# Weights of a hybrid decoder block loaded by 1 MB for two units into two neighbouring slots, instead of 512 KB per unit

## What is computed

```
hn = rms_norm(h, mix_norm_w)
q, k, v, z, xbc, dt, gates = split(hn @ w_in)      # 2048, 2048, 2048, 4096, 6144, 64, 4096 columns
attn = causal attention of 16 heads of 128, q and k normalised per head, ALiBi bias
ssm  = causal conv of width 4 on xbc, SiLU, chunked SSD scan (2 chunks of 128), D skip, gated group RMSNorm with SiLU(z)
h = h + (sigmoid(g_a) * (attn @ w_attn_out) + sigmoid(g_s) * (ssm @ w_ssm_out)) @ w_out
h = h + relu(rms_norm(h, mlp_norm_w) @ w_up)^2 @ w_down      # 8192 wide
```

## Time and profile before

| | us |
|---|---|
| median of three runs | 2007.39 (2006.86 to 2008.67) |
| the profiled execution, its own time | 2008.35 |
| its span, first to last instruction | 2006.6 |
| TensorE busy (matmul) in it | 2000.7 |
| VectorE busy | 1271.5 |
| ScalarE busy | 1103.1 |
| GpSimd busy | 189.7 |

### The profile page before, as it was taken

One profiled execution on the slowest core, in us unless ns is written; L12 is line 12 of the kernel. 1 busy time (PEld: TensorE's weight loads), 2 busy tenths in 40 slices (PEclk: granted clock), 3 DMA queues, 4 the chain that ended last, 5 costly groups with the idle time before them and its releaser, 6 DMA issues.

```text
span 2006.6 us, 25425 instructions
## 1 busy us (share of the span) xinstructions
PE 2000.7 (100%) x9022; PEld 1659.7 (83%) x9022; DVE 1271.5 (63%) x1455; ACT 1103.1 (55%) x1250; POOL 189.7 (9%) x190
## 2 busy tenths in 40 slices
PE   9999999999999999999999999999999999999999
PEld 7888888888888888888888888888888888888887
DVE  5676676777787666666675565656546555655554
ACT  6665666667766454545774444555445435544542
POOL 2110120112221111110000000010001000000000
PEclk9999999999999999999999999999999999999999
DMA  7787887789976666665986766767666766766775
GB/s 246 204 203 197 215 205 201 215 229 240 246 218 191 193 193 197 190 197 178 231 233 197 212 203 233 211 199 211 209 194 202 225 196 191 227 202 188 212 222 164
DMA packets 324282, 417.34 MB, mean 208 GB/s; under 512 B 138832, under 2 KB 139792, under 8 KB 323936
## 3 DMA queue, kind: packets, MB, share of 16 engines
q1 hardware_dynamic: 322768, 412.62, 71.0%
q10 hardware_dynamic: 960, 2.75, 0.4%
q0 software_dynamic: 464, 0.77, 0.2%
HBM read 382.46 MB, written 2.16 MB: 192 GB/s over the span
## 4 chain that ended last, share of the span: by engine, by line
PE 99%; DMA 0%; ACTq 0%; DVE 0%; DVEq 0%; issue 0%
PE ps L610 32%; PE ps L612 32%; PE ps L611 32%; PE ps L793 1%; PE ps L579 0%; PE ps L655 0%; PE ps L678 0%; PE ps L782 0%; DMA x_in<-in_x 0%; PE ps L803 0%; PE ps L679 0%; PE ps L656 0%; PE ps L699 0%; PE ps L701 0%; PE ps L586 0%; PE ps L587 0%
## 5 line engine op out<-in xcount | busy, mean ns | idle before, releaser
L1437 DVE TENSOR_TENSOR wlo<-raw,whi 128x1024 fp32r<-128x1024 f32 x703 | 886.7, 1268 | 631.6 <-ACT whi L911 630.1
L911 ACT ACTIVATE whi<-raw 128x1024 fp32r<-128x1024 f32 x703 | 738.8, 1058 | 682.1 <-PE ps L612 663.2
L610 PE MATMUL ps<-whi,xT_hi 128*128 128x512 f32 x1276 | 505.6, 396 | 0.0
L612 PE MATMUL ps<-whi,xT_lo 128*128 128x512 f32 x1276 | 497.4, 390 | 0.0
L611 PE MATMUL ps<-wlo,xT_hi 128*128 128x512 f32 x1276 | 496.6, 389 | 0.0
L612 PEld LDWEIGHTS ps<-whi,xT_lo 128*128 128x128 f32 x1276 | 239.4, 188 | 50.8
L611 PEld LDWEIGHTS ps<-wlo,xT_hi 128*128 128x128 f32 x1276 | 239.8, 188 | 49.1 <-issue 1.0
L610 PEld LDWEIGHTS ps<-whi,xT_hi 128*128 128x128 f32 x1276 | 239.7, 188 | 48.7 <-issue 1.1
L610 PE MATMUL ps<-whi,hT_hi 128*128 128x512 f32 x512 | 199.3, 389 | 0.0
L612 PE MATMUL ps<-whi,hT_lo 128*128 128x512 f32 x512 | 199.2, 389 | 0.0
L610 PE MATMUL ps<-whi,fT_hi 128*128 128x512 f32 x512 | 199.2, 389 | 0.0
(11 more groups left out here) (263 smaller groups left out, 1907.7 us busy)
## 6 DMA issues: line engine op xcount, KB each, us to landing
raw<-in_w_in SPq DMA_DIRECT2D x319, 512.0 KB, 4.1
raw<-in_w_up SPq DMA_DIRECT2D x128, 512.0 KB, 4.3
raw<-in_w_down SPq DMA_DIRECT2D x128, 512.0 KB, 4.2
raw<-in_w_ssm_out SPq DMA_DIRECT2D x64, 512.0 KB, 4.3
raw<-in_w_attn_out SPq DMA_DIRECT2D x32, 512.0 KB, 4.3
raw<-in_w_out SPq DMA_DIRECT2D x32, 512.0 KB, 4.4
arow<-arows SPq DMA_DIRECT2D x16, 512.0 KB, 4.8
h<-in_x ACTq DMA_DIRECT2D x1, 2048.0 KB, 10.9
```

The source lines that it names most:

```text
L610: mm(dst, xh, whi[sl][:, kk, :], start=(s == 0 and kk == 0), stop=False)
L612: last = mm(dst, xl, whi[sl][:, kk, :], start=False, stop=(s == US - 1 and kk == UK - 1))
L911: A(whi[s % SLOTS][:, :, :], raw[s % SLOTS][:, :, :], ACT.Copy).then_inc(hi_ready, 1)
L1437: V.tensor_tensor(wlo[s % SLOTS][:, :, :], raw[s % SLOTS][:, :, :], fp(whi[s % SLOTS][:, :, :]), ALU.subtract).then_inc(lo_ready, 1)
```

## The change

The four raw slots become one tensor, `raw_all`, and `raw[s]` a view of it. In `load_block` only the even s issue a transfer: 4 tiles of 128 rows, 1 MB, for the slots of s and s + 1. It waits for a `lo_ready` one higher than the single load of s did, that is until VectorE has read both slots; the single load of s + 1 had waited for just this value. Each pair of slots has one semaphore, and ScalarE waits for it at both units. What stands behind an s in the queue (the turns) stays behind that s.

At the start the first unit is still loaded in two halves, now with a semaphore for each; unit 1 stays a load of 512 KB; units 2 and 3 come in one transfer, ahead of the second of SyncE's three pieces of x.

```
-        raw = [sb(f"raw{s}", "RAW", 4096 * s, [P, UK, COLS]) for s in range(SLOTS)]
+        raw_all = sb("raw_all", "RAW", 0, [P, SLOTS * UK, COLS])
+        raw = [raw_all[:, s * UK:(s + 1) * UK, :] for s in range(SLOTS)]
...
-        raw_in = [sem(f"raw_in{s}") for s in range(SLOTS)]
-        half_in = sem("half_in")
+        raw_in = [sem(f"raw_in{s}") for s in range(SLOTS // 2)]
+        half_in = [sem(f"half_in{s}") for s in range(UK)]
...
                 for s in range(SLOTS if isinstance(b, int) and b == 0 else 0, US):
-                    sp.wait_ge(lo_ready, US * b + s - SLOTS + 1)
-                    src = w[bass.ds(row0 + s * UK * P, UK * P), bass.ds(col0, COLS)]
-                    sp.dma_start(raw[s % SLOTS][:, :, :], src.rearrange("(k p) n -> p k n", p=P)) \
-                        .then_inc(raw_in[s % SLOTS], 16)
+                    if s % 2 == 0:
+                        sp.wait_ge(lo_ready, US * b + s - SLOTS + 2)
+                        src = w[bass.ds(row0 + s * UK * P, 2 * UK * P), bass.ds(col0, COLS)]
+                        sp.dma_start(raw_all[:, (s % SLOTS) * UK:(s % SLOTS + 2) * UK, :],
+                                     src.rearrange("(k p) n -> p k n", p=P)).then_inc(raw_in[(s % SLOTS) // 2], 16)
...
             for s in range(1, SLOTS):
-                sp.dma_start(raw[s][:, :, :],
-                             w_in[s * UK * P:(s + 1) * UK * P, Q0:Q0 + COLS].rearrange("(k p) n -> p k n", p=P)) \
-                    .then_inc(raw_in[s], 16)
+                if s < 3:
+                    n = s * UK
+                    sp.dma_start(raw_all[:, n:2 * n, :],
+                                 w_in[n * P:2 * n * P, Q0:Q0 + COLS].rearrange("(k p) n -> p k n", p=P)) \
+                        .then_inc(raw_in[s - 1], 16)
...
-                act.wait_ge(raw_in[s % SLOTS], 16 * ((US // SLOTS) * b + s // SLOTS + 1))
+                act.wait_ge(raw_in[s % SLOTS // 2], 16 * ((US // SLOTS) * b + s // SLOTS + 1))
```

More of the change, by code:

```diff
@@ L501, in _ @@
                 sp.dma_start(raw[0][:, kk, :], w_in[kk * P:(kk + 1) * P, Q0:Q0 + COLS]) \
-                    .then_inc((half_in, raw_in[0])[kk], 16)
+                    .then_inc(half_in[kk], 16)
             for s in range(1, SLOTS):
-                sp.dma_start(raw[s][:, :, :],
-                             w_in[s * UK * P:(s + 1) * UK * P, Q0:Q0 + COLS].rearrange("(k p) n -> p k n", p=P)) \
-                    .then_inc(raw_in[s], 16)
+                if s < 3:
[3 more added lines that the diff above has]
+                        .then_inc(raw_in[s - 1], 16)
                 sp.dma_start(x_in[:, :, s * COLS:(s + 1) * COLS],
@@ L946, in _ @@
             x_hi(0)((0,))
-            act.wait_ge(half_in, 16)
+            act.wait_ge(half_in[0], 16)
             A(whi[0][:, 0, :], raw[0][:, 0, :], ACT.Copy).then_inc(half_hi, 1)
             x_hi(0)((1,))
-            act.wait_ge(raw_in[0], 16)
+            act.wait_ge(half_in[1], 16)
             A(whi[0][:, 1, :], raw[0][:, 1, :], ACT.Copy).then_inc(hi_ready, 1)
```

## The result

The changed kernel takes 2049.11 us (median of four runs, 2045.64 to 2054.26), the kernel before 2007.84 us beside it. The ratio is 1.021, with a 95% interval of 1.0197 to 1.0223: 41 us slower. The prediction said 2012.2 us, range 2007.6 to 2016.8; the measured slowdown is nearly nine times the 4.8 us that it forecast. The four times lie in two pairs, 2045.64 and 2045.74 at a mean granted clock of 0.995 and 0.996, 2052.48 and 2054.26 at 0.992.

The account below looks back on a forecast made before the run. TensorE, busy 2000.7 of 2006.6 us, was taken as the bound. Start 0.3, k's transposes 4.2 and x's second load 0.3 summed to 4.8 us, giving 2012.2 from the median of 2007.39; range 2007.6 to 2016.8.

Parts of the forecast that it names:

- Bytes and count: Weight loads: same bytes in half as many transfers; a pair lands whole after 4.9 us at best, 5.5 median.
- The steady stream: Weight loads after the start: the even unit's later load just fits before its release; cost 0.
- TensorE's margin of 5.9 us: Weight units: time between wlo being done and TensorE needing the unit, taken to cover late pairs.
- The even unit's 5.9 us: Weight loads: three units, 8.2 us, between releases less 2.3 us until wlo frees the slot; landing takes 4.9 to 5.5.
- The four k places: Scores after k's transposes: TensorE waits for kT, 2.4 us first and 0.6 at three others; 4.2 in all.
- L: Landing time of k's second transpose behind 512 KB more: bounds 5.9 and 7.1 us, taken as 6.5.
- The start: First block: units 2 and 3 land together, so TensorE waits 0.3 us ahead of unit 2; bounds 0 and 0.6.
- x again: Second load of x on ScalarE's queue: the pair beside it comes late, wait 0.3 us, upper bound 1.5.
- the convolution: Conv's second transpose: VectorE waits 1.5 us in each of eleven blocks, inside the margin; cost 0.
- rival 2: Conv blocks and y's also make TensorE wait, 1 us a block, +11, 2023 us; chance 0.12.
- Rival 3: Weight stream starves if a pair takes twice a single's time, 8.2 us: +140, 2150 us; chance 0.01.
- The signs of being wrong: Profile after: steady-stream TensorE waits at whi or wlo, pairs landing in 7 us or more, or k joins waiting no longer.

Follow-up runs that it names:

- e4: Changed kernel with VectorE writing M one unit earlier, ahead of the wlo of step 3, in eight SSD blocks: 2029.18 us, ratio 1.0112.
- e8: Kernel before with only units 2 and 3 of the first block loaded in one transfer: 2008.3 us, ratio 1.0005.
- e2: Changed kernel's wait and queue order, but each pair as two 512 KB loads with separate landings, start as before: 2019.21 us, ratio 1.0059.
- e1: Kernel before with 512 KB loads kept, only each even unit's load waiting one unit of wlo longer: 2020.63 us, ratio 1.0065.
- e7: Kernel with the pair's wait and two 512 KB loads, but ScalarE waits for both before rounding the first unit: 2053.1 us, ratio 1.023.
- e9: Pair's wait with two separately landing 512 KB loads, plus k's transposes both behind s = 3 and M one unit earlier: 2008.38 us, ratio 1.0004.
- e5: Changed kernel with both repairs, k's transposes behind s = 3 and M ahead of the late unit: 2014.52 us, ratio 1.0036.
- e3: Changed kernel with both transposes of k behind s = 3, ahead of the pair of s = 4: 2040.88 us, ratio 1.0173.

## Why the prediction was wrong

- **Bytes and count: right in the median,** a pair lands in 5.2 us (predicted 5.5); too slow at best, 3.8 (4.9).
- **The steady stream, "Cost: 0": the step that failed.** "It just fits, and if it is late TensorE's margin of 5.9 us stands behind it" is true of weights and was put in for everything. In blocks 40 to 87 it held exactly. The window of the changed kernel that answers to the earlier trace rows, 2517 matmuls against 2516:

```profile
1370.00:1940.00 570.00, 570.00 (x2517) 472.12 (x2516) 315.06 (x280) 276.11 (x267) 20.85 (x11) 1.00 0.68 206
```

  Elsewhere the stream is not what has the least margin. An engine's queue is one line, and what stands behind a late unit is late with it: M with 0.6 us of cover, kT with 1.3. The prediction followed this chain for the transposes and never for the SSD blocks. They hold 22 of the 37 us of the profiled execution; e4 shows it.
- **What it overlooked to get there.** The even unit's 5.9 us from slot free to release was counted from a wlo that follows its rounding at once. Where VectorE has other work, wlo came 3.3 us late (684.62 to 687.91) before the pair was issued. Before, the even unit had 2.7 us more, and that covered it: ScalarE's 663 us of waiting for TensorE (now 411) were this slack.
- **The four k places: right mechanism, under-sized.** Predicted 2.4 + 3 x 0.6 = 4.2 us; the waits are 4.60 and 1.3 to 1.5, 8.8 in all, and with the clock and further delays the stretch costs 13. Of the first, the landing was at my low bound (5.9), but the lateness that reached it was 3.6 us where I took 1.0 with a bound of 1.9. With both, my own sum gives 0.8 + 3.6 = 4.4. (Over the four places a transpose landed in 5.9 to 6.9 us, 6.2 in the median, where I took L = 6.5.) In the second place L was at the high bound: 165.72 - 158.75 = 7.0, for which the sum gives 1.1 and 1.41 was measured. In the third it was 238.88 - 232.87 = 6.0, which gives 0.1; the 1.54 came of a transpose issued 1.25 us later than counted (at 232.87; 222.20 and the 9.42 us by which the whole is late there make 231.62). Lateness of that kind I had counted in the first place alone.
- **The clock: missing.** Each wait was priced at its own length. About 8 us more came of it in the profiled execution, about 16 in two of the others.
- **The start and x again: right; the convolution: small, but not 0.** Unit 2 waited 0.28 us (0.3 predicted), e8 finds none of it in the total; x's second load cost 0 (0.3). The convolution blocks cost 2.5 us (0, rival 2 had 11), all in blocks 20 to 23, where the one wait of TensorE for a rounded unit falls (1.0 us).
- **Rival 3, the starving stream, had the mechanism half:** raw did come late, 133 times, but TensorE did not wait for it.
- **The signs of being wrong** looked in the wrong place as well. None came up: 1.0 of TensorE's 25 us of waits was at whi, a pair landed in 5.2 us and not 7, the joins of k waited 4.2 us each and not 1. None of the three looks at what stands behind a unit of weights in VectorE's queue.

Two causes of lateness are told apart by the runs: with the repairs absent, later issue alone costs 12 to 13 us (e2, e1) and waiting for both units 30 to 34 more (e2 against the changed kernel and e7). Part of these 30 to 34 is the lower clock that came with the waits: e2's was 0.999, the other two had 0.990 to 0.996. With the repairs present the two are 0 and 6 (e9, e5). What stays open is whether e1's queue order makes all of its 5 us in the convolution, and which of the waits bring the clock down.

## What to carry to other kernels

When a transfer gets coarser, price two delays for every small unit in it: the later issue (the last slot must be free) and the later use (the last byte must be there). Then hold the sum not against the margin of the units themselves, but against the smallest cover of anything that stands behind a unit in any engine's queue, and look first where that engine has just come from other work. A wait that can't be avoided should stand behind its neighbours in the queue rather than ahead: moving one instruction of eight blocks ahead of the late unit gave back 20 us here and cost nothing. And compare more than the profiled execution where waits are long: here executions of one kernel lay 8 us apart with the clock.

## What the runs showed of the hardware

TensorE's granted clock fell from 2.4 to 1.2 GHz (1.00 to 0.50) at 92.0 us, 3 us into the wait of 4.60 us, and TensorE was at work for some 5 us, from 93.6, before it was back at 98.9 (windows above). Behind the wait of 2.54 us in block 28 it fell at 699.6, when TensorE was at work again; windows of the changed kernel:

```profile
698.00:700.00 2.00, 1.04 (x8) 1.05 (x8) 2.00 (x2) 0.00 (x0) 0.00 (x0) 0.90 0.34 124
700.00:702.00 2.00, 2.00 (x11) 2.00 (x11) 0.04 (x1) 0.26 (x1) 0.00 (x0) 0.50 0.41 56
702.00:704.00 2.00, 2.00 (x6) 1.61 (x6) 1.17 (x1) 0.80 (x1) 1.72 (x2) 0.50 0.97 359
704.00:706.00 2.00, 2.00 (x6) 1.52 (x6) 1.00 (x2) 0.00 (x0) 1.30 (x1) 0.50 0.32 125
706.00:708.00 2.00, 2.00 (x10) 1.59 (x9) 0.00 (x0) 1.00 (x1) 0.00 (x0) 0.89 0.00 0
```

It fell a third time behind a wait of only 1.45 us that ended at 752.7 (0.56 and 0.59 from 754 to 758 us), and not at all behind waits of 2.50 and 2.63 us, at 594.5 and 806.3. Of twelve waits in the two kinds of places three had this. What one fall costs is seen from two blocks with nearly the same wait: block 24 (2.50 us, no fall) lost 2.8 us, block 28 (2.54, a fall of 6.8 us) lost 6.1. In all the profiles the six longest waits, 3.11 to 5.04 us (the changed kernel, e2, e3, e4 twice, e7), had a fall each; of the shorter ones some had and most had not, so their length alone doesn't tell. The Trainium skill (TensorE: Matmul & The Clock Gate, Why this matters for your kernels) names long idle gaps between bursts of matmuls as what lowers the clock; the six longest waits agree with that, and the falls behind 2.54 and 1.45 us show that shorter gaps can be followed by one as well.

A transfer of 1 MB landed 5.2 us after its issue in the median, one of 512 KB 4.1. The Trainium skill's advice to batch to 1 MiB (DMA: Bandwidth & Descriptors, under Bandwidth) agrees with that as a rate for one transfer (1 MB in 5.2 us is 202 GB/s, 512 KB in 4.1 are 128). The packets of SyncE's queue also took less of the 16 engines' time, 66.5% of 2044.0 us against 71.0% of 2006.6, for the same 412.6 MB. In the time of the kernel nothing of it is gained, as the transfers were not what TensorE waited for before; and e7, with 512 KB and the same waits, is as slow as the changed kernel.
